# A state-space mixer with its skip term in the step matrix, tokens in the order step, chunk, and all copies between its layouts on ScalarE

## The reference

```python
u = h @ w_in
# 64 groups of 16 channels; each group has 64 complex states x
# x[t] = a * x[t-1] + B u[t];   y[t] = Re(C x[t])
y = y + d_skip * u                 # the skip term, one factor per channel
g = gelu(y)
val, gate = split(g @ w_glu)
return val * sigmoid(gate)
```

## Time and profile before

| | |
|---|---|
| median of 3 runs | 2051.86 us (2051.42 to 2054.62) |
| profiled execution, its own time | 2057.72 us |
| its span in the trace | 2055.9 us |
| TensorE busy | 1976.9 us, 96% |
| VectorE busy | 1222.1 us, 59% |
| ScalarE busy | 844.1 us, 41% |
| GpSimd busy | 442.2 us, 22% |
| mixer stage: first spreading piece to last `a_lo` | 675.3 to 808.7 us in the trace |

### The profile page before, as it was taken

The page is one execution under the profiler, slowest core; times in us unless marked ns, Lnnn a source line. Parts: engine busy times, 40 slices in busy tenths (PEclk is TensorE's granted clock), DMA queues, the critical chain, the costliest instruction groups (busy, mean ns, idle before and its releaser), DMA issues.

```text
span 2055.9 us, 26447 instructions
## 1 busy us (share of the span) xinstructions
PE 1976.9 (96%) x9640; PEld 1606.6 (78%) x9640; DVE 1222.1 (59%) x1723; ACT 844.1 (41%) x1287; POOL 442.2 (22%) x609
## 2 busy tenths in 40 slices
PE   8999999999999897999999999999878999999998
PEld 7999678888887786877887887777666777877887
DVE  5345456474554897467557466744666676365565
ACT  4322332122224796344324244544655444243242
POOL 3110019998934453100000001100000200000010
PEclk9999799999999999999999999999989999999999
DMA  4322023254452332322322323232111223223232
GB/s 147 95 74 66 29 82 95 90 201 152 164 195 92 108 131 95 103 72 92 113 79 91 107 82 116 92 106 74 52 52 37 63 91 103 89 95 104 81 123 93
DMA packets 65076, 201.64 MB, mean 98 GB/s; under 512 B 6422, under 2 KB 19222, under 8 KB 63948
## 3 DMA queue, kind: packets, MB, share of 16 engines
q1 hardware_dynamic: 57372, 166.39, 24.7%
q0 software_dynamic: 7600, 33.84, 4.6%
HBM read 184.44 MB, written 15.77 MB: 97 GB/s over the span
## 4 chain that ended last, share of the span: by engine, by line
PE 85%; DVE 7%; ACT 5%; issue 2%; DMA 1%; POOL 1%; SPq 0%; DVEq 0%; ACTq 0%; POOLq 0%
PE ps L451 61%; PE ps L590 6%; PE ps L1749 5%; PE ps L741 2%; PE ps L440 1%; PE ps L816 1%; ACT t L2063 1%; PE ps L1981 1%; DVE w_lo L430 1%; DMA cp<-mix_cp 1%; PE ps L1868 1%; ACT w_hi L426 1%; POOL t L532 1%; DVE t L2016 1%; PE ps L1808 1%
## 5 line engine op out<-in xcount | busy, mean ns | idle before, releaser
L430 DVE TENSOR_TENSOR w_lo<-raw,w_hi 128x1024 fp32r<-128x1024 f32 x308 | 397.7, 1293 | 172.7 <-ACT w_hi L426 172.3
L451 PE MATMUL ps<-x_hi,w_hi 128*128 128x512 f32 x1152 | 459.0, 398 | 4.0 <-DVE w_lo L430 2.6
L451 PE MATMUL ps<-x_lo,w_hi 128*128 128x512 f32 x1152 | 455.7, 396 | 0.0
L451 PE MATMUL ps<-x_hi,w_lo 128*128 128x512 f32 x1152 | 453.5, 394 | 0.0
L426 ACT ACTIVATE w_hi<-raw 128x1024 fp32r<-128x1024 f32 x308 | 322.2, 1049 | 248.5 <-DMA raw<-in_wstream 162.0
L451 PE MATMUL ps<-a_hi,w_hi 128*128 128x512 f32 x704 | 278.1, 395 | 2.9 <-DVE w_lo L430 2.9
L451 PE MATMUL ps<-a_hi,w_lo 128*128 128x512 f32 x704 | 277.8, 395 | 0.0
L451 PE MATMUL ps<-a_lo,w_hi 128*128 128x512 f32 x704 | 277.8, 395 | 0.0
L451 PEld LDWEIGHTS ps<-x_hi,w_hi 128*128 128x128 f32 x1152 | 216.5, 188 | 69.1 <-issue 11.5
L532 POOL TENSOR_TENSOR t<-t,sq 128x512 f32<-128x512 f32 x49 | 72.7, 1484 | 919.1 <-ACT sq L523 917.1
L451 PEld LDWEIGHTS ps<-x_hi,w_lo 128*128 128x128 f32 x1152 | 216.7, 188 | 49.7
(11 more groups left out here) (401 smaller groups left out, 3019.9 us busy)
## 6 DMA issues: line engine op xcount, KB each, us to landing
raw<-in_wstream SPq DMA_DIRECT2D x308, 512.0 KB, 3.3
ev<-mix_ev POOLq DMA_DIRECT2D x8, 1024.0 KB, 5.1
mix_cp<-c_p POOLq DMA_DIRECT2D x8, 640.0 KB, 3.4
cp<-mix_cp POOLq DMA_DIRECT2D x8, 640.0 KB, 6.4
mix_ev<-v_b POOLq DMA_DIRECT2D x8, 512.0 KB, 3.5
fall<-fall POOLq DMA_DIRECT2D x4, 544.0 KB, 5.1
h<-in_xT SPq DMA_DIRECT2D x4, 528.0 KB, 7.0
mix_ev<-e_r POOLq DMA_DIRECT2D x1, 2048.0 KB, 9.5
```

The costliest lines, as they stand in the source:

```text
L430: e.tensor_tensor(w_lo[:, u.slot, :], raw[:, u.c % 2, :], w_hi[:, u.slot, :], ALU.subtract)\
L451: last = e.matmul(ps[:, bank, :], wt[:, u.slot, w], x[:, k0 + k, 0:SEQ], start=(k == 0 and n == 0), stop=(k == kt - 1 and n == 2))
```

## The change

The tokens' order changes, the copies change engine, and the skip term moves.

- Tokens are in the order step, chunk from `st_u` on: VectorE writes `st_u` (and, behind the second product, `t1` in `glu_dve`, which turns the order back) through a view in which neighbouring results lie far apart or four elements apart. Each spreading and gathering piece now reads and writes 128 neighbouring elements.
- All 16 spreading and all 16 gathering pieces of a tile are ScalarE's. `spread_pool` and `mixer_back_pool` are gone.
- The skip term is added to the step matrix by four matmuls of 32 by 32 a tile, from a diagonal `d_mat` that GpSimd makes (`diagonal_pool`). `mixer_out_dve` and semaphore `ys_ok` are gone; GELU reads PSUM bank 7, and TensorE's next use of that bank waits for the GELU (`ge_ok`).

```diff
     def spread_at(m, q, j):
-        src = st_u[32 * q:32 * q + 32, m % 2, :].rearrange("p (c j) -> p j c", j=4)[:, j:j + 1, :]
+        src = st_u[32 * q:32 * q + 32, m % 2, j * P:(j + 1) * P].unsqueeze(1)
...
+    def diagonal_pool(e, m):
+
+        ge(e, g_mm, m - 1)
+        d = vecs[0:32, COL["ssm_d"] + 4 * m:COL["ssm_d"] + 4 * m + 4].unsqueeze(2).to_broadcast([32, 4, 32])
+        e.tensor_tensor(d_mat[:, m % 2, :, :], ident[0:32, 0:32].unsqueeze(1).to_broadcast([32, 4, 32]), d, ALU.mult)\
+            .then_inc(dm_ok, 1)
...
         ge(e, tl_ok, 4 * m)
+        e.wait_ge(dm_ok, m + 1)
...
+            last = e.matmul(ps[0:32, 6, q * P:q * P + 32], d_mat[:, b, q, :], ident[0:32, 0:32], start=False, stop=True)
...
-        e.wait_ge(ut_a, 10 * m + 10)
-        e.wait_ge(ut_p, 6 * m + 6)
+        e.wait_ge(ut_a, 16 * m + 16)
...
     def mixer_back_pe(e, m):
-        ge(e, ys_ok, 4 * m)
+        ge(e, ge_ok, m)
...
     def mixer_back_act(e, m):
-        e.wait_ge(ys_ok, 4 * m + 4)
+        e.wait_ge(y_mm, m + 1)
         g = u_t[:, 4 * m:4 * m + 4, :].rearrange("p q c -> p (q c)")
-        e.activation(g, g, ACT.Gelu_apprx_tanh).then_inc(ge_ok, 1)
+        e.activation(g, ps[:, 7, :], ACT.Gelu_apprx_tanh).then_inc(ge_ok, 1)
...
     def glu_dve(e, u, m):
-        e.tensor_tensor(t1[:, m % 2, 0:SEQ], ps[:, u.slot, :], t0[:, m % 2, 0:SEQ], ALU.mult).then_inc(unit_ev, 1)
+        by_step = lambda t: t.rearrange("p (j c) -> p j c", j=4)
+        e.tensor_tensor(t1[:, m % 2, 0:SEQ].rearrange("p (c j) -> p j c", j=4), by_step(ps[:, u.slot, :]),
+                        by_step(t0[:, m % 2, 0:SEQ]), ALU.mult).then_inc(unit_ev, 1)
...
-                e.tensor_tensor(st_u[:, i % 2, :], ps[:, i % 2, :], rstd[:, 0:SEQ], ALU.mult).then_inc(unit_ev, 1)
+                by_time = lambda t: t.rearrange("p (c j) -> p c j", j=4)
+                e.tensor_tensor(st_u[:, i % 2, :].rearrange("p (j c) -> p c j", j=4), by_time(ps[:, i % 2, :]),
+                                by_time(rstd[:, 0:SEQ]), ALU.mult).then_inc(unit_ev, 1)
...
-            if i >= 2:
-                mixer_out_dve(e, i - 2)
```

More of the change, by code:

```diff
@@ L232, in build @@
         st_u = sb("st_u", [P, 2, SEQ], F32, c)
+        d_mat = sb("d_mat", [32, 2, 4, 32], F32, c)
         rstd_f = sb("rstd_f", [P, SEQ], F32, c)
@@ L357, in build @@
     ut_a = sem("ut_a")
-    ut_p = sem("ut_p")
     par_v = sem("par_v")
@@ L379, in build @@
     y_mm = sem("y_mm")
-    ys_ok = sem("ys_ok")
+    dm_ok = sem("dm_ok")
     ge_ok = sem("ge_ok")
     un_a = sem("un_a")
-    un_p = sem("un_p")
     g_hi = sem("g_hi")
@@ L1310, in mixer_tables_pe @@
         ge(e, tl_ok, 4 * m)
+        e.wait_ge(dm_ok, m + 1)
         for q in range(4):
             for k in range(2):
-                last = e.matmul(ps[0:32, 6, q * P:(q + 1) * P], V_B[b][:, k, q, 3, :, :].rearrange("p g c -> p (g c)"),
-                                C_P[m % 3][:, k, q, 0:4, :, :].rearrange("p j g c -> p (j g c)"),
-                                start=(k == 0), stop=(k == 1))
+                e.matmul(ps[0:32, 6, q * P:(q + 1) * P], V_B[b][:, k, q, 3, :, :].rearrange("p g c -> p (g c)"),
+                         C_P[m % 3][:, k, q, 0:4, :, :].rearrange("p j g c -> p (j g c)"),
+                         start=(k == 0), stop=False)
+            last = e.matmul(ps[0:32, 6, q * P:q * P + 32], d_mat[:, b, q, :], ident[0:32, 0:32], start=False, stop=True)
         last.then_inc(g_mm, 1)
@@ L1354, in mixer_front_act @@
             e.activation(t_l[32 * j:32 * j + 32, m % 2, :, 32 * j:P], g[:, :, 0:P - 32 * j], ACT.Copy).then_inc(tl_ok, 1)
-    POOL_PIECES = ((0, 2), (1, 3), (2, 2), (3, 3), (1, 2), (0, 3))
-    ACT_PIECES = [(q, j) for q in range(4) for j in range(4) if (q, j) not in POOL_PIECES]
+    PIECES = [(q, j) for q in range(4) for j in range(4)]
     def spread_act(e, m):
-        for q, j in ACT_PIECES:
+        for q, j in PIECES:
             dst, src = spread_at(m, q, j)
             e.activation(dst, src, ACT.Copy).then_inc(ut_a, 1)
[L1364 to L1368, removed]
     def gather_at(m, q, j):
-        return (sq[32 * q:32 * q + 32, m % 2, 0:SEQ].rearrange("p (c j) -> p j c", j=4)[:, j, :],
+        return (sq[32 * q:32 * q + 32, m % 2, j * P:(j + 1) * P],
                 u_t[32 * j:32 * j + 32, 4 * m + q, :])
     def mixer_back_act(e, m):
-        e.wait_ge(ys_ok, 4 * m + 4)
+        e.wait_ge(y_mm, m + 1)
         g = u_t[:, 4 * m:4 * m + 4, :].rearrange("p q c -> p (q c)")
-        e.activation(g, g, ACT.Gelu_apprx_tanh).then_inc(ge_ok, 1)
+        e.activation(g, ps[:, 7, :], ACT.Gelu_apprx_tanh).then_inc(ge_ok, 1)
         e.wait_ge(ge_ok, m + 1)
         ge(e, g_lo, m - 1)
-        for q, j in ACT_PIECES:
+        for q, j in PIECES:
             dst, src = gather_at(m, q, j)
             e.activation(dst, src, ACT.Copy).then_inc(un_a, 1)
-        e.wait_ge(un_a, 10 * m + 10)
-        e.wait_ge(un_p, 6 * m + 6)
+        e.wait_ge(un_a, 16 * m + 16)
         e.activation(a_hi[:, m, :], sq[:, m % 2, 0:SEQ], ACT.Copy).then_inc(g_hi, 1)
[L1388 to L1395, removed]
     def rotation(m):
@@ L1417, in mixer_states_dve @@
         e.drain().then_inc(xs_ok, 1)
[L1419 to L1423, removed]
     def mixer_lo_dve(e, m):
@@ L2249, in _ @@
         e.wait_ge(m4_ok, 1)
+        diagonal_pool(e, 0)
         for m in range(KT):
-            ge(e, ut_p, 6 * m)
             decay_pool(e, m)
+            if m + 1 < KT:
+                diagonal_pool(e, m + 1)
             e.wait_ge(m4_ok, m + 2)
-            e.wait_ge(unit_ev, U_SSM + m + 1)
-            spread_pool(e, m)
             if m == 0:
@@ L2263, in _ @@
                     cp_load(e, m + 1)
[L2264 to L2268, removed]
         e.wait_ge(g_lo, 8)
```

3 lines of the change are left out of this document (1 added, 2 removed).

## The result

| | before | changed |
|---|---|---|
| median of the first comparison | 2054.0 us (6 runs, 2051.42 to 2058.44) | 2062.4 us (6 runs, 2059.29 to 2066.59) |
| profiled execution, its own time | 2057.72 us | 2059.29 us |
| its span | 2055.9 us | 2057.5 us |
| TensorE, VectorE busy | 1976.9, 1222.1 us | 1981.8, 1216.2 us |
| ScalarE, GpSimd busy | 844.1, 442.2 us | 853.1, 393.6 us |

The ratio is 1.0038, 95% interval 1.0023 to 1.0052. Three later series gave 1.0037 [1.0024, 1.0050], 1.0034 [1.0021, 1.0047] and 1.0032 [1.0018, 1.0046]. The mean, 1.0035, is 7.2 us. So the change makes the kernel slower, where no change was forecast, and 2062.4 lies above the range.

A forecast was written before the change was run, and what follows sets the result against it. VectorE and the transfer loop were taken to set the mixer's pace, ScalarE close behind and the bound after the change; terms 1.3 + 0.7 + 0.4 - 2.6 + 0 + 0.45 = +0.25 gave 2052 us, range 2046.5 to 2059.

The forecast's parts named there:

- rival A: Mixer as summed: ScalarE becomes the bound, a piece costs 0.305 to 0.34 us, change -2.6 to +4 us; chance 0.55.
- term 4: Tile 7, spreading to output product: pieces +0.6, VectorE no longer 2.08 late, one L1422 (1.1) gone; -2.6 us in all.
- 1, tiles 0 to 2: Mixer's start: tile 0's spreading 0.6 longer, two `st_u` 0.9 longer, VectorE beside no GpSimd pieces -0.2; +1.3 us.
- 2, tile 2 to 3: First turn with a gather: two groups of pieces 0.6 longer each, a wait for tables absorbs 0.5; +0.7 us.
- 3, four turns: Mixer loop from tile 3 to 7: ScalarE's turn 15.17 against a pace of 15.08, four turns at +0.09; +0.4 us.
- 4 to 6, tile 7 to the unit in `glu`: Tile 7 -2.6 us, mixer's end hidden behind second-product units 0, first stepped `glu_dve` write on the path +0.45.
- 0.299 + 0.02 = 0.32: ScalarE's neighbouring copy piece: length from a 128 by 128 SBUF copy plus spacing, 0.32 us; bounds 0.287 and 0.455.
- TensorE's four products in the step matrix: Mixer's four f32 products of 32 by 32 a tile: 0.5 us taken, bounds 0 and 1.0, TensorE's turn 13.8.
- `st_u` +0.45: VectorE's `st_u` write, now stepped by 512 bytes, takes 0.45 us longer; bounds 0 and 0.75.
- Rival B: Cheap or overlapping pieces, 0.29 us or less: transfer loop binds at 14.6 a turn; -4.5 us, 2047; chance 0.2.
- Rival D: Stepping was free and 0.43 is the cost of copying to other partitions: +26 us, 2078; chance 0.07.
- Rival C: ScalarE's pieces get less cheap, deciding from 0.34 us on: +5 at 0.345, +8 at 0.36, 2057 to 2062; chance 0.18.

The follow-up runs named there:

- warm: Changed kernel plus useless matmuls in TensorE's three long waits (tile 2's tables, tile 7's states, `glu`'s fifth unit); three series: 1.0021, 1.0037, 1.0020 times the kernel before.
- skip_only: Kernel before with only the skip term moved into the step matrix, stepped pieces shared 10 ScalarE, 6 GpSimd; 2056.06 us, 1.0006 times the kernel before.
- order_only: Kernel before with only the tokens' order changed, pieces shared 10 ScalarE, 6 GpSimd, skip term on VectorE; 2052.51 us, 1.0000 times the kernel before.
- share1: Changed kernel with one of a tile's 16 pieces each way given to GpSimd; 2060.15 us, 1.0016 times the kernel before.
- stepped_allact: Changed kernel with tokens in the old order, so all 32 pieces on ScalarE are stepped; 2087.18 us, 1.0161 times the kernel before.
- again2: Changed kernel timed again with no edit, in a later series; 1.0034 times the kernel before.
- again3: Changed kernel timed again with no edit, in the last later series; 2062.74 us, 1.0032 times the kernel before.
- share6: Changed kernel with 6 of a tile's 16 pieces each way given back to GpSimd; 2051.48 us, 0.9979 times the kernel before.

## Why the prediction was wrong, step by step

The mechanism of rival A held: ScalarE becomes the bound, it waits for nothing in a turn, and the last tile gets shorter. From its spreading to its output product the last tile took 21.40 before and 20.54 in the changed kernel (778.31 to 798.85), and 18.82 in all three traces with useless matmuls, where the forecast was 18.8: term 4 was right but for the clock. The sum came out at +0.25 and is +7.4 in the traces (mean of four changed ones) and +7.2 in the timed runs. By the sum's terms:

| term | forecast | changed | with full clock (mean of warm) |
|---|---|---|---|
| 1, tiles 0 to 2 | +1.3 | +1.6 | +1.6 |
| 2, tile 2 to 3 | +0.7 | +2.8 | +1.6 |
| 3, four turns | +0.4 | +1.6 | +1.65 |
| 4 to 6, tile 7 to the unit in `glu` | -2.15 | -0.4 | -1.7 |
| behind it | 0 | +1.9 | -0.2 |
| sum | +0.25 | +7.4 | +3.0 |

- **The step that failed: "The sum over the stage" has no term for TensorE's clock.** It left what TensorE does behind its waits at the price of rows at full clock; tile 7's states stay at 2.05 in term 4. In the changed kernel the states' wait at tile 7 grows from 1.66 to 5.46, and in all four of its traces they take 3.78 to 3.79. The useless matmuls in the three places together take 4.4 us out of the changed kernel's traces: 1.2 between tiles 2 and 3, 1.2 at tile 7, 2.0 behind `glu`'s wait. That is what the lower level costs the changed kernel in its traces, and it isn't all brought by the change, since the kernel before has the lower level too, at 696.00 and at 746.93. Only at tile 7 do all traces agree: each one with a wait of 4.66 or more there has the lower level behind it, each one without such a wait has 2.05. At `glu` skip_only and order_only show that the wait's length doesn't settle it. In the timed runs useless matmuls give 1.9 us, plus or minus 2, and the mean granted clocks leave an estimated 2.1 of the 7.2 to the clock. So the missing term is shown, and its share of the measured loss stays open.
- **The rows for it could have been read beforehand.** The window ahead of tile 2's tables had 0.91 in the kernel before, and the output's products behind a wait of 2.71 there, at 696.00, took 0.63 for two instructions where later ones took 0.39. In the earlier trace rows L1313 took 3.27 behind a wait of 1.42 and 1.93 in another turn; the prediction took the difference off ("so 29.9 without that") and didn't ask what it was.
- **The piece, "0.299 + 0.02 = 0.32", was mis-sized.** It is 0.308 long and 0.33 apart. By the prediction's own rule, 10 ns are 1.9 us, and share1 (14.83) and stepped_allact (19.48) both fit a turn of n x piece + 4.93. Term 3 was +1.6 for +0.4 through this: 32 x 0.01 x 4 = 1.3. Even with 0.33 the forecast would have been +2.2, which is within the range and 5 short.
- **TensorE's four products in the step matrix** were taken at 0.5 a tile and cost 1.0: in the timeline an L1320 group with its L1323 pair lies 0.73 apart, so 16 of L1320 and 8 of L1323 take 3.0 (776.29 to 779.27) where 16 of L1313 took 1.93. It is on the path where ScalarE waits for the tables at tile 2 (1.06 even at full clock), and not in the turns.
- **`st_u` +0.45** was +0.37, and `glu_dve` +0.4: right in size. The Trainium skill's "Vector Engine (DVE) Microarchitecture Reference", section "Measured stream behaviour on trn2", gave an estimate of 0.34 to 0.74, whose lower end this meets.
- **PSUM bank 7 costs nothing**: right but for short waits of the output for the GELU, beside ScalarE's bound: one of 1.22 us in this trace, of tile 5's output, and one more of 1.22 for tile 4's in again2 and again3.

```profile
772.58 0.46 PE L1344 MATMUL ps<-u_t,t_l 128*128 128x128 f32 x2 [1.22 <-ACT u_t L1378]
```

- **Rival B** (overlap of pieces, by "ScalarE: Activation LUTs", section "What ACT_TABLE_LOAD costs", of the Trainium skill) fell: 16 neighbouring pieces of 307 ns take 5.28, so none overlaps. **Rival D** (stepping free) fell: 428 ns stepped and 307 neighbouring, which agrees with the Trainium skill's "SBUF — State Buffer", section "Door 1: The DMA port swizzle (why `[64,N]` ≈ `[32,N]`)". **Rival C** named the right side, "decides from 0.34 on", but the piece stayed below that point and the loss came nonetheless: the side was right by luck, for another reason than the one given. Rival B's sum counts 64 pieces ahead of tile 3 where the forecast's own list has 48, which makes it -4.1 and not -4.5; nothing else hangs on it.

What remains between the full-clock column and the forecast is 2.8 us: 1.9 is the piece, 0.3 to 0.5 the tables at tile 2; the rest wasn't taken apart. That column too is counted against the one trace of before, in whose mixer the clock was low twice.

The shortest account is that of the experiments. Each of the two rewrites alone changes nothing that can be told; both together, with the pieces still shared, are 0.2% faster (share6); moving GpSimd's twelve pieces of a tile onto ScalarE then costs 0.6%, since 12 x 0.33 = 4 us a turn go to an engine that had 11.5 us of work in a turn of 14.13 there, so 2.6 to spare. So 15.48 - 14.13 = 1.35 of a turn is lost. That TensorE or the transfers bind at 14.1 is read from ScalarE's waits and wasn't tested by itself.

## What to carry to other kernels

When several engines stand within a microsecond of one another, price what the change puts on the one that takes the work, and leave work on an idle engine that costs it about the same: GpSimd's 12 pieces lay beside ScalarE's, and share6 shows that keeping them there is 0.6% faster here. Where a change lengthens a wait of TensorE, look at the granted clock behind the waits that the trace already has, and carry the price of the lower level in the range. Ask the same of the kernel before: a gain from a full clock in the new kernel is not the part of the loss that the change brought. A number by which the sum moves 2 us for 10 ns is measured alone first, or the range covers its error.

## What the runs showed of the hardware

- The same 16 matmul instructions of 128 by 128 (8 f32 products) took 2.05 us behind a wait of 1.66 or behind useless matmuls with 0.37 idle, and 3.79 behind a wait of 5.46; in the 8 us window there the granted clock was 0.62, with useless matmuls 1.00. It is not fixed for a program: the same wait ahead of tile 2's tables (2.57 and 2.68) left 0.82 in one execution of the changed kernel and 1.00 in another, and ahead of `glu`'s fifth unit a wait of 2.88 left 0.76 in skip_only and one of 3.28 left 1.00 in order_only.
- ScalarE copies 32 partitions by 128 f32 in 307 ns with neighbouring elements and in 428 to 434 with one side stepped by 16 bytes, 0.94 to 0.98 ns an element; copies follow each other at 0.02 more than their length and don't overlap.
- VectorE writes a product of 128 by 512 from PSUM in 686 ns to neighbours and in 1058 to a step of 512 bytes (`st_u`); behind `glu` the one with a step of 16 bytes took 1071.
- GpSimd copied the same neighbouring pieces, six in a row beside ScalarE's, in 302 ns (spreading) and 381 (gathering) in share6 and in 430 and 415 in order_only, and stepped ones in 629 and 493 in the kernel before.
- VectorE's product of two SBUF arrays ahead of the scan (L1116 and L1117 before, the rows with output `t` and input `t`) took 768 and 844 ns beside GpSimd's stepped pieces, 693 and 685 with no pieces on GpSimd, 702 and 705 beside GpSimd's neighbouring ones in share6 and 736 and 730 in order_only, and 714 and 870 beside stepped ones in skip_only. The pair together is slowest beside stepped copies in both comparisons; more than that these runs don't tell apart.
